# Expert weights and their diagonal matrices move from ScalarE to VectorE, two slots behind the dot product, with eight matrices instead of four

## What is computed

```python
def chunk(xc):
    q = (xc @ w_query).astype(f32).reshape(PEER_CHUNK, PEER_HEADS, 2, PEER_HALF)
    s = jnp.einsum('thcd,hckd->thck', q, keys)
    top_s, top_i = lax.top_k(s, PEER_TOPK)
    ...
    best_s, best_j = lax.top_k(cand_s, PEER_TOPK)
    idx = jnp.take_along_axis(cand_i, best_j, axis=-1)
    gate = jax.nn.softmax(best_s, axis=-1)
    act = jax.nn.gelu(jnp.einsum('thkd,td->thk', u_table[idx].astype(f32), xc.astype(f32)), approximate=False)
    return jnp.einsum('thk,thkd->td', gate * act, v_table[idx].astype(f32)).astype(xc.dtype)
```

## Time and profile before

| | us |
|---|---|
| median of 3 runs | 3679.93 |
| lowest and highest | 3677.33, 3681.28 |
| profiled execution | 3671.43 |
| its span | 3669.6 |

### The profile page before, as it was taken

The page is one execution under the profiler, slowest core; times in us unless marked ns, Lnnn a source line. Parts: engine busy times, 40 slices in busy tenths (PEclk is TensorE's granted clock), DMA queues, the critical chain, the costliest instruction groups (busy, mean ns, idle before and its releaser), DMA issues.

```text
span 3669.6 us, 35899 instructions
## 1 busy us (share of the span) xinstructions
PE 2489.2 (68%) x9537; PEld 1056.4 (29%) x9537; DVE 2214.0 (60%) x4967; ACT 1008.8 (27%) x3376; POOL 1336.4 (36%) x1237
## 2 busy tenths in 40 slices
PE   7999567537656856685676667666756675676576
PEld 4555335413211411141133114111411241132121
DVE  5223240465785677568657855775686568557854
ACT  1111020123233323332322233233323322332222
POOL 1000030024443444444444444444444444444442
PEclk8888665769878877887888679778967886888799
DMA  4111111359999999999999999999999999999998
GB/s 153 44 46 40 43 34 57 148 210 416 419 380 387 419 406 375 411 413 404 376 421 418 377 392 417 417 377 396 416 406 383 413 415 388 407 421 414 388 422 349
DMA packets 192640, 1212.71 MB, mean 330 GB/s; under 512 B 28952, under 2 KB 35416, under 8 KB 51688
## 3 DMA queue, kind: packets, MB, share of 16 engines
q0 software_dynamic: 156672, 1140.92, 76.6%
q1 hardware_dynamic: 35416, 69.28, 5.4%
q10 hardware_dynamic: 320, 0.07, 0.0%
HBM read 1194.51 MB, written 15.55 MB: 330 GB/s over the span
## 4 chain that ended last, share of the span: by engine, by line
DMA 29%; PE 21%; DVE 15%; issue 11%; ACT 5%; POOL 1%; SPq 0%; DVEq 0%; POOLq 0%; ACTq 0%; PEldq 0%
DMA uv_ring<-in_uv_table,idx 28%; PE ACC L1782 12%; PE TQ L1737 6%; DVE uv_ring L1625 4%; DVE S L1589 2%; DVE picks L1590 2%; DVE S L1588 2%; POOL uv_ring L1364 1%; ACT dg L1458 1%; PE OP L1718 1%; ACT dot L1451 1%; DMA wq<-in_w_query 1%; ACT dot L1441 1%; PE ACC L1772 0%; DVE pos L1520 0%
## 5 line engine op out<-in xcount | busy, mean ns | idle before, releaser
L1782 PE MATMUL ACC<-uv_ring,dg 128*64 128x512 f32 x4352 | 1464.7, 784 | 939.4 <-ACT dg L1458 934.8
L1364 POOL DMA_INDIRECT uv_ring<-in_uv_table,idx x1088 | 1262.3, 1160 | 1880.9 <-PE ACC L1782 1350.6
L1625 DVE CUSTOM_DVE_ANT_0 uv_ring<-uv_ring,xn 128x1024 f32<-128x1024 f32 x1088 | 1325.2, 1226 | 819.4 <-DMA uv_ring<-in_uv_table,idx 753.1
L1782 PEld LDWEIGHTS ACC<-uv_ring,dg 128*64 128x64 f32 x4352 | 341.0, 165 | 1944.1 <-ACT dg L1458 1412.5
L1441 ACT ACTIVATE dot<-dot 128x2 f32<-128x2 f32 x544 | 110.5, 203 | 1761.0 <-DVE dot L1625 1748.5
L1458 ACT ACTIVATE dg<-stack,dot 128x64 f32<-128x64 f32 x1088 | 328.5, 341 | 53.3
L1737 PEld LDWEIGHTS TQ<-glu_and_queries,wq 128*128 128x128 f32 x2304 | 267.5, 195 | 66.3 <-issue 64.1
L1737 PE MATMUL TQ<-glu_and_queries,wq 128*128 128x128 f32 x2304 | 281.6, 281 | 2.0 <-DMA wq<-in_w_query 1.9
L1451 ACT ACTIVATE dot<-gate,dot 128x1 f32<-128x1 f32 x1088 | 261.3, 287 | 17.8
L503 PE MATMUL PJ<-w_in,xT 128*128 128x512 f32 (+1 forms) x432 | 157.9, 525 | 1.7 <-DMA w_in<-in_w_in 1.7
L503 PEld LDWEIGHTS PJ<-w_in,xT 128*128 128x128 f32 x432 | 82.6, 192 | 78.8 <-issue 73.5
(11 more groups left out here) (318 smaller groups left out, 1927.4 us busy)
## 6 DMA issues: line engine op xcount, KB each, us to landing
uv_ring<-in_uv_table,idx POOLq DMA_INDIRECT x1088
glu_and_queries<-in_w_glu SPq DMA_DIRECT2D x9, 1024.0 KB
wq<-in_w_query SPq DMA_DIRECT2D x1, 8192.0 KB, 33.4
xt<-in_x SPq DMA_DIRECT2D x9, 512.0 KB, 3.4
xr<-scratch_x SPq DMA_DIRECT2D x9, 512.0 KB
w_in<-in_w_in SPq DMA_DIRECT2D x2, 2048.0 KB, 10.8
xk<-in_x SPq DMA_DIRECT2D x8, 512.0 KB, 3.3
scratch_x<-xk SPq DMA_DIRECT2D x8, 512.0 KB, 2.6
```

What stands on the lines that cost most here:

```text
L1364: pool.indirect_dma_start(out=ring[:, s_ % RING, :], out_offset=None, in_=a["uv_table"], in_offset=bass.IndirectOffsetOnAxis(ap=idx[:, s_: ...
L1625: V.tensor_tensor_reduce(row, row, xn[:, g, :], 1.0, 0.0, ALU.mult, ALU.add, dot[:, s_:s_ + 1]).then_inc(dots, 1)
L1782: ins = nc.tensor.matmul(ACC[GT * g:GT * (g + 1), b, :], dg[:, n % DG, :], ring[:, n % RING, D + 512 * b:D + 512 * b + 512], start=False, ...
```

## The change

`weigh` and `diagonal` go from ScalarE's list, with the semaphore between them. ScalarE keeps the GELU, and `begin` with it shrinks to one `activate`. VectorE gets `diagonals`: for a batch, one wait for ScalarE's GELU and two operations that each make a matrix, `stack` times the GELU column times the gate column. They stand behind the second product of the *next* batch, so two slots behind. The last batch of a turn comes behind the first two products of the next turn and ahead of `sum_out`, the first batch of a turn behind product 3. `DG` goes from 4 to 8, one matrix for each place of the ring, and the wait on `pv` ahead of a matrix goes.

```diff
-        KS, NSLOT, RING, DG, BATCH, LEAD = TOPK, EH * TOPK, 8, 4, 2, 3
+        KS, NSLOT, RING, DG, BATCH, LEAD = TOPK, EH * TOPK, 8, 8, 2, 3
...
-                def weigh(t, s_):
-
-                    if s_ == 0:
-                        k["gate_ready"].of(act, t)
-                    elif s_ == EARLY:
-                        k["gate_rest"].of(act, t)
-                    act.wait_ge(gelus, t * (NSLOT // BATCH) + s_ // BATCH + 1)
-                    for n in range(s_, s_ + BATCH):
-                        ins = A(wgt[:, n:n + 1], gate[:, n:n + 1], ACT.Copy, scale=act_w[:, n:n + 1])
-                    ins.then_inc(wgts, 1)
-                    act.wait_ge(wgts, t * (NSLOT // BATCH) + s_ // BATCH + 1)
-
-                def diagonal(t, s_):
-
-                    act.wait_ge(pv, t * NSLOT + s_ + 1 + RING - DG)
-                    A(dg[:, s_ % DG, :], stack[:], ACT.Copy, scale=wgt[:, s_:s_ + 1]).then_inc(diags, 1)
-
...
                         activate(t, b)
                         if last:
                             take_rows(t + 1, 1)
-                        weigh(t, b)
                         for s_ in range(b, b + BATCH):
-                            diagonal(t, s_)
                             if prep := prepared(turn, t, s_):
                                 prepare(*prep)
                     if turn != "samples":
-                        begin(t + 1)
+                        activate(t + 1, 0)
...
+                def diagonals(t, s_):
+
+                    if s_ == 0:
+                        k["gate_ready"].of(dve, t)
+                    elif s_ == EARLY:
+                        k["gate_rest"].of(dve, t)
+                    dve.wait_ge(gelus, t * (NSLOT // BATCH) + s_ // BATCH + 1)
+                    for n in range(s_, s_ + BATCH):
+                        V.scalar_tensor_tensor(dg[:, n % DG, :], stack[:], act_w[:, n:n + 1], gate[:, n:n + 1].to_broadcast([P, GT]),
+                                               ALU.mult, ALU.mult).then_inc(diags, 1)
+
...
                     for s_ in range(LEAD, slots_of(turn)):
                         product(t, s_)
+                        if s_ % BATCH == BATCH - 1:
+                            diagonals(t, s_ + 1 - 2 * BATCH)
...
                     if turn != "samples":
                         for s_ in range(LEAD - 1):
                             product(t + 1, s_)
+                    diagonals(t, slots_of(turn) - BATCH)
                     sum_out(t, n, t * NSLOT + slots_of(turn))
```

More of the change, by code:

```diff
@@ L1288, in retrieve_experts @@
         pv = c.sem("v_used")
-        gelus, wgts, diags = c.sem("gelus"), c.sem("weights_done"), c.sem("diags_done")
+        gelus, diags = c.sem("gelus"), c.sem("diags_done")
         dch = PerTile(c.sem("dve_steps_e"), DVE_STEPS)
@@ L1477, in retrieve @@
                     if turn != "samples":
-                        begin(t + 1)
+                        activate(t + 1, 0)
                     root_out(t, NS_ROWS if turn == "samples" else P)
-                def begin(t):
-                    activate(t, 0)
-                    weigh(t, 0)
-                    for s_ in range(BATCH):
-                        diagonal(t, s_)
                 for n in ("y_gelu yT_done gate_y sd_y_done sd_x_done xnT_done qT_a qT_b qT_c qT_d S_a S_b ex_done "
@@ L1498, in _ @@
                     prepare(1, 0, j)
-                begin(0)
+                activate(0, 0)
                 with act.Fori(0, PT - 1) as t:
```

## The result

| | median us | ratio to before, 95% |
|---|---|---|
| before (4 runs beside it) | 3680.61 | |
| after | 4014.39 | 1.0907 (1.0888 to 1.0926) |

The account below looks back on a forecast made before the run. The bound was taken to be when TensorE releases a ring slot, since its next gather can't be issued before. Six terms, 22 + 20 + 8 + 36 + 32 + 20 = 138 us on 3671.4, gave 3815 us, range 3715 to 3935.

Parts of the forecast that it names:

- ring bound everywhere: Rival, chance 0.17: a gather needs 8 to 8.5 us, so every ring trip is 1 to 2 us longer; 3880 to 3980.
- F: Calm stretches at TensorE's slow clock, outside the picks: 0.2 us each time round the ring, 20 us (0 to 85).
- the spare of 1.3 or -0.2 us: Time an even slot's gather has left to land after the change, beyond its 6.75 us, at fast or slow clock.
- The release: Odd product's start to GpSimd's next gather: 5.4 us (6.9 slow clock) before, 9.4 (10.9) after, 4.0 later.
- The gather's need: Time from issue to use with nothing queued ahead: 6.75 us, from a gather behind the loop's branch.
- A: GpSimd's loop branch at the end of a turn: everything moves by 3.7 us at six branches, 22 us.
- D: Slot 22, VectorE's residual add waiting for TensorE's w_bot projection: 4.5 us a turn (2 to 6), 36 us.
- B: End of a turn, later last and first matrices: slot 10 used 2.5 us later (0 to 5), 20 us over eight turns.
- C: Slot 13, VectorE waiting for TensorE's transposes of y behind matrices just issued: 1 us (0 to 3), 8 in all.
- E: Picks, where VectorE is full, and batches ahead: 0.4 us per batch, 4.0 us a turn, 32 us (22 to 60).
- the lower DMA rate: Sign expected in the new profile: DMA rate below 403 GB/s.
- the picks: Sign expected in the new profile: two slots take 6.3 to 6.5 us there, against 5.96 before.

Follow-up runs that it names:

- The work alone: Kernel before with two further 128x64 VectorE operations in each batch, written to a spare tile nobody reads, ScalarE's order unchanged: 3706.44 us (1.0074).

## Why the prediction was right in its sign and wrong in its size

**Half of the mechanism was right**: the release of a ring place moved back by 4 us, and VectorE's work cost little. But the forecast had DMA keep its floor in calm stretches, and it does not. The time lies above the range's 3,935. The rival "ring bound everywhere", with 0.17, is what happened; its 3880 to 3980 were too low as well.

**The step that failed is F**, the calm stretches, put at 20 us (0 to 85). Slots 32 to 79 lost 9.5 us a turn, 76 in all, and the samples' turn 26.6 more: 103 us where neither a branch nor a named wait stands. F rests on the spare of 1.3 or -0.2 us, and that on the two terms that follow, the second above all.

**The release.** Said: 5.4 us from the odd product to the even place's gather, 6.9 at the slow clock, and 4.0 later after the change. In the kernel before this interval has a mean of 7.2 us and a first decile of 5.44 (384 batches, slots 0 to 95): the batch of the earlier trace rows that I called undisturbed is among the fastest tenth. After, it is 11.5 (said: 9.4, or 10.9 at the slow clock). So the shift of 4.3 was right, both ends were 2 us too early for the fast clock, and those for the slow clock were close.

**The gather's need.** Said: 6.75 us. That is a gather behind the branch, with one other on its way (the six of the kernel before took 5.5 to 6.8 us); with two on their way the median is 8.1 to 8.2. With both, 19.9 less 11.5 less 2.5 leaves 5.9 us to land where 8.1 are needed. **The spare is about -2 us, not +1.3 or -0.2.** The rival's argument was right too that gathers land sooner with fewer queued (the median over slots 0 to 95 fell from 11.9 to 9.4 us), but not by enough. By the Trainium skill's rule on one DMA (DMA: Bandwidth & Descriptors, in the section on the anatomy of one DMA) the estimate was 4.4 us, which is still further off: the shortest in the trace of the kernel after is 5.34.

Further, TensorE's 3.65 us for eight matmuls in the samples' turn, where both slots of a batch go to the same half of the sum (1.94 in the earlier trace rows, at the full clock too), was not in the sum at all. Nor was a clock that falls because of the change: the mean of the stretch is 0.75 against 0.79.

**A** (branch): said 22, measured 21, uncertain by 16 (what the change adds to the branch's cost). **D** (slot 22): said 36, measured 34, uncertain by 13, in the kernel after, and nothing before. With such errors that they agree to 2 us is in part luck. The rows of turn 2, the answer to the earlier trace rows:

```profile
1607.37 3.70 PE L1706 MATMUL OP<-w_bot,yT_and_cand 128*128 128x512 f32 x8
...
1613.78 3.70 PE L1706 MATMUL OP<-w_bot,yT_and_cand 128*128 128x512 f32 x8
...
1617.71 0.69 DVE L1530 TENSOR_TENSOR xr<-OP,xr 128x512 f32<-128x512 f32 x1 [3.76 <-PE OP L1706]
...
1620.37 1.22 DVE L1599 CUSTOM_DVE_ANT_0 uv_ring<-uv_ring,xn 128x1024 f32<-128x1024 f32 x1
...
1626.49 1.27 POOL L1364 DMA_INDIRECT uv_ring<-in_uv_table,idx  x1 [9.69 <-PE ACC L1770]
...
1632.35 1.22 DVE L1599 CUSTOM_DVE_ANT_0 uv_ring<-uv_ring,xn 128x1024 f32<-128x1024 f32 x1 [5.00 <-DMA uv_ring<-in_uv_table,idx]
```

VectorE waits 3.76 us (3.4 to 6.7 over turns 0 to 7, 5 to 8 forecast), but it comes late itself; the price is behind it, at slot 28, where it waits 5.00 us for a gather that GpSimd, idle for 9.69 us, could not issue sooner.

**B** (end of a turn): said 2.5 us. The answer to the earlier trace rows, from a turn that starts at 1541.91:

```profile
1550.05 1.23 DVE L1616 COPY S<-ACC 128x1024 f32<-128x1024 f32 x1 [3.45 <-PE ACC L1770]
...
1560.24 1.23 DVE L1599 CUSTOM_DVE_ANT_0 uv_ring<-uv_ring,xn 128x1024 f32<-128x1024 f32 x1 [4.98 <-issue]
...
1561.93 3.68 PE L1770 MATMUL ACC<-uv_ring,dg 128*64 128x512 f32 x8 [8.62 <-DVE dg L1609]
...
1566.38 1.65 POOL L1364 DMA_INDIRECT uv_ring<-in_uv_table,idx  x1 [13.04 <-PE ACC L1770]
...
1572.53 1.23 DVE L1599 CUSTOM_DVE_ANT_0 uv_ring<-uv_ring,xn 128x1024 f32<-128x1024 f32 x1 [3.75 <-DMA uv_ring<-in_uv_table,idx]
...
1579.05 1.23 DVE L1599 CUSTOM_DVE_ANT_0 uv_ring<-uv_ring,xn 128x1024 f32<-128x1024 f32 x1 [0.26 <-DMA uv_ring<-in_uv_table,idx]
```

Slot 8's gather is asked for 24.5 us after the turn's start (20.4 in the prediction's chain, 10.1 before), slot 10 used after 37.1 (32.2 and 29.6). Product 3 came 2.4 us later than said, 1.9 of them at the copy, and from TensorE's start to the release it took 4.5 us, not 2.7, since TensorE had idled for 8.62 us and worked at the lower clock. Slots 0 to 15 lose 7.7 us a turn, and slot 10 is late by about as much here. Part of that can be the branch's. **C** (slot 13): VectorE waits 2.6 to 4.8 us for the transposes where it waited 0.2 to 1.3, near the 3 to 5 forecast; it was not tried apart.

**E** (picks): 0.4 us per batch was right. One head to the next, against 5.96 in the earlier trace rows, is 6.36, and the medians of all such pairs are 5.97 and 6.36:

```profile
1824.64 1.19 DVE L1562 TENSOR_TENSOR S<-place,pos_f 128x992 f32<-128x992 f32 x1
1831.00 1.19 DVE L1562 TENSOR_TENSOR S<-place,pos_f 128x992 f32<-128x992 f32 x1
```

Slots 96 to 111 lose 4.6 us a turn, 37 in all; 32 were said for these and the batches ahead of them. The work alone costs 27 to 29.

Of the 334 us then: some 21 branch, 34 slot 22, 29 VectorE's work. Some 250 are left, a remainder and not a measured part, that B, C and F had at 48. Of it the calm stretches above are 103.

Of the signs put down ahead of the result, the lower DMA rate, the picks and the longer wait at slot 13 came true. Turns took 379 us instead of 355 to 360, and gathers were used 9.4 us after issue on the median instead of 6 to 8.

## What to carry to other kernels

With a ring of buffers, write down the loop: from a transfer's issue over every engine to the release that lets the next transfer be issued, and count how many places it advances. If an engine's own wait for a later transfer stands inside, the places behind that wait are lost: eight became six here, and a single product ahead of two small operations cost 263 us of 334. Take the release from the mean of many rows and not from one that looks calm. Take the landing from rows with as many transfers on their way as the changed kernel will have: the plain median of the kernel before (11.9 us) is mostly queue and costs nothing, its row behind the branch (6.75) had one gather ahead, and rows with two ahead (8.1 us) stood in the same trace. A spare that is the small difference of two favourable rows is no spare.

## What the runs showed of the hardware

- A gather of 128 rows of 8 KB took, from issue to use and where it was waited for, 5.3 us at the least, and on the median of the two kernels' traces 6.5 and 7.8 us with one earlier gather on its way, 8.1 and 8.2 with two, 9.5 and 9.2 with three, 11.3 and 11.5 with four.
- Behind a loop's branch GpSimd was idle for 7.3 to 10.7 us ahead of its next gather, against 0.3 to 4.0 with the loop written out. The six branches cost 21 us (14 to 27) with spare in the ring and 42 (27 to 57) without.
- A pair of VectorE's 128x64 operations with two per-partition factors takes 0.48 us, although each is recorded at 280 ns.
- TensorE's lower clock was part of a circle: TensorE idled because the ring was late, its granted clock went from 0.99 to 0.86 in the samples' turn, and its sum, part of the ring's loop, took 6.13 us from its start to the next gather instead of 3.56. Two more matmuls a batch brought the clock of that turn back to 0.99.
